# Expert loop of a streaming encoder step: next expert's gate product ahead of this one's down product, lo halves on VectorE alone

## The reference, cut to what matters

```python
def expert_block(args):
    xb, e = args
    return (jax.nn.silu(xb @ w_g[e]) * (xb @ w_u[e])) @ w_d[e]
```

## Time and profile before

| what | value |
|---|---|
| median of 3 runs | 1662.56 us (1661.34 to 1664.23) |
| span of the profiled execution | 1662.2 us |
| TensorE busy | 1306.2 us (79%) |
| VectorE busy | 1166.7 us (70%) |
| ScalarE busy | 694.7 us (42%) |
| GpSimd busy | 925.6 us (56%) |
| moved by DMA | 279.76 MB, mean 168 GB/s |
| the chain that ended last | TensorE 34%, issue 11%, VectorE 8% of the span |

### The profile page before, as it was taken

One profiled execution on the slowest core, in us unless ns is written; L12 is line 12 of the kernel. 1 busy time (PEld: TensorE's weight loads), 2 busy tenths in 40 slices (PEclk: granted clock), 3 DMA queues, 4 the chain that ended last, 5 costly groups with the idle time before them and its releaser, 6 DMA issues.

```text
span 1662.2 us, 18411 instructions
## 1 busy us (share of the span) xinstructions
PE 1306.2 (79%) x5969; PEld 1043.3 (63%) x5969; DVE 1166.7 (70%) x1171; ACT 694.7 (42%) x833; POOL 925.6 (56%) x829
## 2 busy tenths in 40 slices
PE   1777678887755699906888888888888888886998
PEld 0666567675633588805776666766767666744776
DVE  2279969788878422294887998888888789844442
ACT  2322223333323322212665666666666666622121
POOL 1367739999951300043777777777777777730000
PEclk9998889798766799956999999999999999997999
DMA  5311010000010332122898888889999999963320
GB/s 181 109 51 31 12 57 14 24 10 4 28 51 25 127 127 76 38 102 69 291 312 320 301 307 299 303 306 311 326 317 327 318 321 326 330 219 127 123 81 32
DMA packets 122318, 279.76 MB, mean 168 GB/s; under 512 B 17537, under 2 KB 20033, under 8 KB 122269
## 3 DMA queue, kind: packets, MB, share of 16 engines
q1 hardware_dynamic: 112477, 261.28, 45.4%
q0 software_dynamic: 9792, 17.85, 2.9%
HBM read 269.85 MB, written 27.12 MB: 179 GB/s over the span
## 4 chain that ended last, share of the span: by engine, by line
PE 34%; issue 11%; DVE 8%; ACT 2%; DMA 1%; SPq 0%; DVEq 0%; POOL 0%; POOLq 0%; ACTq 0%
PE ps L407 10%; PE ps L408 10%; PE ps L409 10%; DVE ahl L388 2%; PE ps L1615 2%; DVE mem L1538 1%; PE ps L1966 1%; ACT hhl L1075 1%; PE ps L1928 1%; DMA mem<-y_rows 1%; DVE whl L388 1%; PE ps L1862 1%; PE ps L1938 0%; DVE hhl L388 0%; DMA mem<-in_g_ple 0%
## 5 line engine op out<-in xcount | busy, mean ns | idle before, releaser
L388 DVE TENSOR_TENSOR whl<-mem,whl 128x1280 fp32r<-128x1280 f32 (+1 forms) x205 | 506.8, 2503 | 27.1 <-ACT whl L1052 25.7
L388 POOL TENSOR_TENSOR whl<-mem,whl 128x768 fp32r<-128x768 f32 (+1 forms) x213 | 467.7, 2223 | 103.1 <-ACT whl L385 62.1
L407 PE MATMUL ps<-whl,ahl 128*128 128x512 f32 x1124 | 452.9, 403 | 73.5 <-DVE ahl L388 71.4
L1052 ACT ACTIVATE whl<-mem 128x2048 fp32r<-128x2048 f32 x196 | 375.9, 1919 | 178.5 <-PE ps L409 178.5
L408 PE MATMUL ps<-whl,ahl 128*128 128x512 f32 x1124 | 444.6, 396 | 0.0
L409 PE MATMUL ps<-whl,ahl 128*128 128x512 f32 x1124 | 442.8, 394 | 0.0
L407 PEld LDWEIGHTS ps<-whl,ahl 128*128 128x128 f32 x1124 | 221.5, 197 | 128.6 <-issue 71.9
L409 PEld LDWEIGHTS ps<-whl,ahl 128*128 128x128 f32 x1124 | 219.9, 196 | 45.4
L408 PEld LDWEIGHTS ps<-whl,ahl 128*128 128x128 f32 x1124 | 220.5, 196 | 42.6 <-issue 0.2
L459 DVE SCALAR_TENSOR_TENSOR mem<-mem 128x256 f32<-128x256 f32 (+1 forms) x270 | 199.5, 808 | 0.0
L668 POOL TENSOR_SCALAR mem<-mem 128x1 f32<-128x1 f32 (+1 forms) x54 | 21.5, 397 | 318.8 <-ACT mem L875 286.3
(11 more groups left out here) (234 smaller groups left out, 1415.6 us busy)
## 6 DMA issues: line engine op xcount, KB each, us to landing
mem<-in_w_e_up SPq DMA_DIRECT2D x66, 1024.0 KB, 7.5
mem<-in_w_e_down SPq DMA_DIRECT2D x66, 1024.0 KB, 6.8
mem<-in_w_e_gate SPq DMA_DIRECT2D x66, 1024.0 KB, 5.6
mem<-in_x_prompt SPq DMA_DIRECT2D x24, 512.0 KB, 3.4
mem<-y_rows SPq DMA_DIRECT2D x16, 512.0 KB, 5.6
mem<-in_w_in SPq DMA_DIRECT2D x4, 1024.0 KB, 8.7
mem<-in_w_out SPq DMA_DIRECT2D x4, 1024.0 KB, 4.9
h_rows<-mem SPq DMA_DIRECT2D x8, 512.0 KB, 2.6
```

The source lines that it names most:

```text
L388: return which.tensor_tensor(out, full, hi.bitcast(F32), ALU.subtract)
L407: nc.tensor.matmul(out, act_hi, whl[:, 0, w_at], start=first, stop=False)
L1052: nc.scalar.activation(whl[:, 0, slot * CH:(slot + 1) * CH], raw[c], ACT.Copy).then_inc(s_mhi, 1)
```

## The change

- GpSimd makes no lo halves any more; VectorE makes each whole (128x2048), with one counter, also of the first four chunks, which it makes after the slot table. LOV stays in use in the mixer only.
- The jobs run in another order. The gate chunks of expert 0 come first, then for each expert: its up chunks, the next expert's gate chunks, its own down chunks. TensorE's order in an expert becomes: all transposes of the next slots, up, first half of the next gate product, transposes of the hidden row, second half of that gate product, down.
- The gate product goes to bank 2 and bank 7 in turn.
- ScalarE writes all of y in one operation; one counter s_ye takes the place of s_y0 and s_y1.
- The last expert, which has no next, is written out behind the loop. SP loads the chunks in the new order.

The diff, cut to its core:

```diff
+        JOB_CHUNK = (2, 3, 0, 1, 4, 5)
+        JOB_AHEAD = (0, 0, 1, 1, 0, 0)
+        JOB_BUFFER = (2, 3, 4, 5, 0, 1)
+        LAST_JOB = 2 + 6 * (NE - 1)
+        GATE_BANK = (2, 7)
+        def first_job(e):
+            return 6 * e + 2
...
 # SyncE
-            with sp.Fori(1, NE) as e:
-                for c in range(6):
-                    sp.wait_ge(s_mlv, 6 * e + (c - 5))
-                    sp.wait_ge(s_mlp, 6 * e + (c - 5))
-                    sp.dma_start(raw_view(c), expert_chunk(e, c)).then_inc(s_mraw[c], 16)
+            for i in (4, 5):
+                sp.wait_ge(s_mlv, i - 3)
+                load_job(JOB_BUFFER[i], 0, JOB_CHUNK[i])
+            with sp.Fori(1, NE - 1) as e:
+                for i in range(6):
+                    sp.wait_ge(s_mlv, 6 * e + (i - 3))
+                    load_job(JOB_BUFFER[i], e + JOB_AHEAD[i], JOB_CHUNK[i])
+            for i, c in enumerate((2, 3, 4, 5)):
+                sp.wait_ge(s_mlv, LAST_JOB + i - 5)
+                load_job((LAST_JOB + i) % 6, NE - 1, c)
...
 # GpSimd
-            for c in range(4):
-                pool.wait_ge(s_mhi, c + 1)
-                for first, last, signal in ((0, LOV, s_mlv), (LOV, CH, s_mlp)):
-                    lo_part(nc.gpsimd, whl[:, 1, c * CH + first:c * CH + last], whl[:, 0, c * CH + first:c * CH + last],
-                            raw[c][:, first:last]).then_inc(signal, 1)
...
-                    for c in range(4, 10):
-                        expert_lo(6 * e + c, (6 * b + c) % 4, c % 6)
-                    pool.wait_ge(s_y0, e + 2)
-                    pool.wait_ge(s_y1, e + 2)
+                    pool.wait_ge(s_ye, e + 2)
...
 # ScalarE
+            for n in range(4):
+                expert_hi(n, n, n, 16, None)
             slots_hi(0, 1)
+            expert_hi(4, 0, 4, 16, 1)
+            gate_tanh(0, 2, None)
+            act.sem_inc(s_ye, 1)
+            def one_expert(e, b):
+                slots_hi(1 - b, e + 2)
+                for i in (3, 4, 5):
+                    job_hi(e, b, i)
+                hidden_hi(e + 1)
+                job_hi(e, b, 6)
+                gate_tanh(1 - b, first_job(e) + 4, e + 1)
+                for i in (7, 8):
+                    job_hi(e, b, i)
+                weighted_out(e, b, first_job(e) + 6)
...
 # VectorE
+            for n in range(2):
+                expert_lo(n, n, n)
             slots_lo(0, 1)
+            expert_lo(2, 2, 2)
+            expert_lo(3, 3, 3)
+            gated(0, 1)
+            expert_lo(4, 0, 4)
+            def one_expert(e, b):
+                slots_lo(1 - b, e + 2)
+                job_lo(e, b, 3)
+                hidden(first_job(e) + 2, e + 1)
+                job_lo(e, b, 4)
+                hidden_lo(e + 1)
+                job_lo(e, b, 5)
+                job_lo(e, b, 6)
+                gated(1 - b, e + 2)
+                job_lo(e, b, 7)
+                job_lo(e, b, 8)
...
 # TensorE
+            def one_expert(e, b, gathered):
+                slot_transpose(1 - b, 0, gathered=gathered, evacuated=e + 1)
+                slot_transpose(1 - b, 1)
+                up_products(e, b)
+                pe.wait_ge(s_xsl, e + 2)
+                half_product(first_job(e) + 2, (4 + 2 * b) % 4, GATE_BANK[1 - b], 1 - b, 0)
+                hidden_transpose(e)
+                half_product(first_job(e) + 3, (5 + 2 * b) % 4, GATE_BANK[1 - b], 1 - b, 1)
+                pe.wait_ge(s_hl, e + 2)
+                pe.wait_ge(s_ye, e + 1)
+                for half in range(2):
+                    down_product(first_job(e) + 4 + half, (6 + 2 * b + half) % 4, half)
```

More of the change, by code:

```diff
@@ L1045, in _, with expert_hi, job_hi, last_hi @@
             nc.scalar.activation(e2, mt, ACT.Exp).then_inc(s_rta, 1)
[L1048 to L1052, removed]
+            def expert_hi(n, slot, buffer, arrived, free):
+                act.wait_ge(s_mraw[buffer], arrived)
+                if free is not None:
+                    act.wait_ge(s_use, free)
+                nc.scalar.activation(whl[:, 0, slot * CH:(slot + 1) * CH], raw[buffer], ACT.Copy).then_inc(s_mhi, 1)
+            def job_hi(e, b, i):
+                expert_hi(None, (2 + 2 * b + i) % 4, (2 + i) % 6, 16 * (e + (8 + i) // 6), first_job(e) + (i - 3))
+            def last_hi(n):
+                expert_hi(n, n % 4, n % 6, 16 * (n // 6 + 1), n - 3)
             def slots_hi(b, count):
@@ L1056, in slots_hi, with gate_tanh, hidden_hi @@
                 nc.scalar.activation(ahl[:, b, 0, :], banks2(0), ACT.Copy).then_inc(s_xsh, 1)
+            def gate_tanh(b, products, turned):
+                act.wait_ge(s_use, products)
+                if turned is not None:
+                    act.wait_ge(s_mht, turned)
+                nc.scalar.activation(th, bank(GATE_BANK[b]), ACT.Tanh, scale=0.5).then_inc(s_mth, 1)
+            def hidden_hi(turned):
+                act.wait_ge(s_mht, turned)
+                nc.scalar.activation(hhl[:, 0, :], bank(4), ACT.Copy).then_inc(s_hh, 1)
@@ L1065, in _ @@
-            with act.Fori(0, NE, 2) as e0:
-                for b in range(2):
[L1067 to L1082, removed]
+            expert_hi(4, 0, 4, 16, 1)
@@ L1514, in _, with expert_lo, job_lo, last_lo @@
             nc.vector.tensor_copy(idx_gather.bitcast(I32), tmp48).then_inc(s_tab, 1)
[L1517 to L1520, removed]
+            def expert_lo(n, slot, buffer):
+                dve.wait_ge(s_mhi, n + 1)
+                at = slice(slot * CH, (slot + 1) * CH)
+                lo_part(nc.vector, whl[:, 1, at], whl[:, 0, at], raw[buffer]).then_inc(s_mlv, 1)
+            def job_lo(e, b, i):
+                expert_lo(first_job(e) + i, (2 + 2 * b + i) % 4, (2 + i) % 6)
+            def last_lo(n):
+                expert_lo(n, n % 4, n % 6)
             def slots_lo(b, count):
@@ new lines, in gated, with hidden, hidden_lo @@
+            def gated(b, count):
+                dve.wait_ge(s_mth, count)
+                nc.vector.scalar_tensor_tensor(th, th, 1.0, bank(GATE_BANK[b]), ALU.add, ALU.mult).then_inc(s_mg, 1)
+            def hidden(products, count):
+                dve.wait_ge(s_use, products)
+                dve.wait_ge(s_mg, count)
+                nc.vector.tensor_tensor(th, th, bank(3), ALU.mult).then_inc(s_mh, 1)
+            def hidden_lo(count):
+                dve.wait_ge(s_hh, count)
+                lo_part(nc.vector, hhl[:, 1, :], hhl[:, 0, :], bank(4)).then_inc(s_hl, 1)
@@ L1549, in ovf_block @@
+            with dve.Fori(0, NE - 2, 2) as e0:
+                for b in range(2):
+                    one_expert(e0 + b, b)
+            one_expert(NE - 2, 0)
+            last_lo(LAST_JOB + 3)
+            hidden(LAST_JOB + 2, NE)
+            hidden_lo(NE)
+            for n in range(LAST_JOB + 4, LAST_JOB + 8):
+                last_lo(n)
             def ovf_block(j):
@@ L1916, in ovf_block @@
+                    one_expert(e0 + b, b, 8 * e0 + 16 * (1 + b))
+            one_expert(NE - 2, 0, 8 * NE)
+            up_products(NE - 1, 1)
+            hidden_transpose(NE - 1)
+            pe.wait_ge(s_hl, NE + 1)
+            pe.wait_ge(s_ye, NE)
+            for half in range(2):
+                down_product(LAST_JOB + 2 + half, (LAST_JOB + 2 + half) % 4, half)
             def ovf_block(j):
                 if first_extra(j):
-                    pe.wait_ge(s_xsl, NE + 1)
+                    pe.wait_ge(s_g[0], 16 * (NE // 2 + 1))
```

128 lines of the change are left out of this document (52 added, 76 removed).

## The result

The changed kernel takes 1535.9 us in the median of four runs (1532.9 to 1536.7), against 1662.4 before in the same comparison. The ratio is 0.9236, with a 95% interval of 0.9218 to 0.9254: 7.6% faster.

What follows compares the result with a forecast made beforehand. The prediction took TensorE's waits for late lo halves to limit the loop, with DMA the next bound. From 1662.2: -16.2 routing, +2.3 start, -59.2 loop, +2.6 end, plus 0.4 outside the span, gives 1592 us; range 1560 to 1650.

Steps and rivals of the forecast that it cites:

- 348 GB/s is what a share of 1.0 would move: Expert loop: DMA's ceiling taken as rate over share, from 313 GB/s at a share of 0.90.
- DMA's floor is 19.5 us per expert: Expert loop: 6.78 MB an expert needs 19.5 us of DMA, above TensorE's 18.1.
- 3.38 us a chunk: Expert loop: time per loaded chunk at a DMA share of 0.96; 3.25 us at 1.0.
- a packet takes no longer when much is under way: DMA: rate over share stays constant, 348 in the loop, 344 and 355 in two other stretches.
- rival C: Expert loop: TensorE is the bound, as DMA can move more than 348 GB/s; 1537 us, chance 0.12.
- TensorE's pace: Expert loop: TensorE's own work takes 18.1 us an expert, 72 matmuls 16.5 and twelve transposes 1.6.
- Start: Ahead of the loop: routing gains 16.2 us, a lo operation holding GpSimd's copy costs 2.3; first product at 757.0.
- The start of the load queue: Start of the loop: chunk 12 is in 20 us behind the first product, at 777.6, then 179 chunks follow.
- End: Behind the loop: overflow block's weights queue behind five loads of the last stage, +2.6 us, bounds -2.8 and +6.
- D: Expert loop: period stays at 21.66 us, another wait replacing the two; only 13.9 us won, 1649 us, chance 0.06.
- E: Expert loop: whole lo operation takes 4.14 us, VectorE becomes the bound at 28.1 an expert; 1849 us, chance 0.05.
- B: Expert loop: DMA does not fill, share stays at 0.90, TensorE waits for whl; 1631 us, chance 0.22.

Runs made afterwards that it cites:

- VectorE alone: The kernel before in its old order, but all lo halves made whole on VectorE, none on GpSimd: 1584.5 us, ratio 0.9513.
- less compute: The changed kernel without the experts' hi by lo matmul and with only 256 columns of each lo half made in the loop: 1527.5 us.
- half loads: The changed kernel with each load in SyncE's loop cut to its first half, all other work kept: 1529.1 us.
- the run with the gather first: The changed kernel, VectorE's first two lo halves waiting until GpSimd has issued the first gather and copied the second index: 1529.1 us, ratio 0.9180.
- the routing run: The kernel before, only the first four chunks' lo halves moved from GpSimd to VectorE, whole, behind the slot table: 1653.6 us, ratio 0.9936.
- the fastest version: The changed kernel with the first gather issued first, gate and up chunks loaded in 8 KB pieces, slots turned with a stride: 1521.0 us, ratio 0.9148.

## Why the prediction was wrong

**Where it held.** The mechanism of the gain was right: GpSimd's lo halves cost VectorE more than they took off it. VectorE alone gives 80 us, the whole lo half measured 2.29 us against 2.27 forecast, and the waits for ahl and hhl went, as said. By the port lock that the Trainium skill describes ("SBUF — State Buffer", section "SBUF: two separate sides"), the copy would wait out a whole VectorE operation; the trace agrees: the index copy took 2.17 us behind one lo half of 2.24. That TensorE and DMA would be the next two limits was right too; the forecast had DMA alone in front, by 1.4 us an expert.

**The step that failed** is "348 GB/s is what a share of 1.0 would move", and with it "DMA's floor is 19.5 us per expert" and 3.38 us a chunk. What the runs showed in its place is a ceiling of 382 GB/s (less compute), at a share of 1.02. The step rested on "a packet takes no longer when much is under way". It takes less. In the row of the loads' queue q1, share x 16 engines x 500 us / packets is the time of one packet: 113 ns with half loads (share 0.63 of all queues), 109 before (0.88), 106 with VectorE alone (0.97), 102 in the changed kernel and with less compute (1.02). GpSimd's lo halves are not the reason, as the run with half loads has none. The rows for before and after, 800 to 1300 us (packets, MB, share of 16 engines):

```profile
q1 hardware_dynamic: 60515, 143.59, 82.3%
```

```profile
q1 hardware_dynamic: 73731, 174.49, 94.2%
```

So the share is not a linear measure of what is left: from 0.90 at 313 GB/s the step to full was 22%, not 11%. Two parts of it: a full queue shows a share of 1.02, not 1.0, and rate over share rises from 348 to 375. The three rows whose rate I divided by their share all lay below a full queue. Could the trace of before have shown it? It has stretches of 4 us in which the queue was full, and some of them look like the answer:

```profile
1188.00:1192.00 4.00, 4.00 (x20) 3.25 (x19) 3.60 (x4) 3.09 (x2) 0.92 (x1) 1.00 1.02 383
1348.00:1352.00 4.00, 2.69 (x15) 2.22 (x16) 2.62 (x3) 3.15 (x3) 4.00 (x3) 1.00 1.04 378
```

But the same view has others, and a stretch of 20 us can be found that is full all through:

```profile
1148.00:1152.00 4.00, 3.66 (x20) 2.83 (x18) 2.90 (x4) 2.11 (x2) 3.12 (x6) 1.00 1.01 301
...
1303.00:1323.00 20.00, 18.49 (x87) 15.07 (x86) 15.21 (x12) 14.34 (x11) 16.89 (x9) 1.00 1.01 364
```

Of the 150 stretches of 4 us from 800 to 1400 us, 33 have a share of 1.00 or more; they move 301 to 407 GB/s, 359 in the mean. So the trace of before gave 350 to 365 by this way too. It left room above 348, but did not show 382: that took a run in which DMA is the bound throughout.

With 382, DMA's floor is 6.78 MB / 382 = 17.7 us, below the 18.1 that I gave TensorE, and the sum would have been rival C's. C had a chance of 0.12 because of this one reading. That C's 1537 is about 1 us from the measured median is in part luck. Its end of the loop, 1339, was met (1338.4) because three errors cancel: the first product came 2.4 us later, 32 periods are 7 us shorter together, and what the loop takes beside them is 4 us longer. It has nothing of the 5 us won behind the loop. And TensorE was the bound in two thirds of the loop, not in all of it. Why packets get shorter in a full queue no run settles.

**The page.** I weighed 358 GB/s for a core's part against about 425 for a core that streams alone (the Trainium skill, "HBM Reference", section "Specifications (TRN2)"), and found the rows to agree with the first. Neither fits: 382 with pieces of 2 and 4 KB, 400 with longer ones. The kernel runs on one core alone, which is the case the page gives the second figure for; I let my quotient overrule that.

**Terms that were off by less.** TensorE's pace: 18.1 forecast, 17.68 measured (half loads). I took 0.229 us a matmul from a stretch with small pauses and 1.6 for the twelve transposes, which take 0.87 + 0.44 = 1.3 in the changed kernel. Start: -13.9 forecast, -11.5 measured. The routing stretch gave 16.1, as forecast (16.2), and the changed kernel came to it 0.6 us earlier. But I let one lo operation hold the copy (+2.3) and put a late gather outside the sum; both came, 5.2 together, beyond my bound of 4.6. The copy agrees with the page's lock, and the slower issue is VectorE's doing; whether the rest is the starving of which the page warns or the loads in front of the gather is open, as the run with the gather first says. The start of the load queue has a slip: 20 us behind 757.0 is 777.0, not 777.6. End: +2.6 forecast, -3.0 measured. The overflow weights were asked for at 1335.1, when the five PLE loads, issued by 1323.7, had had 11 us; the block's first product then waited for ScalarE's copy and not for weights. That the forecast had a queue there comes in part from the same wrong ceiling; the routing run won 3 us at this place too, with the old order, so not all of the term is explained.

**D and E.** No wait took the place of the removed two; the whole lo half stayed far below 3.1 us. B's share of 0.90 never came.

## What to carry to other kernels

Rate over share at part load is no ceiling: here it was 9% too low, and the short full stretches of the same trace were too scattered to correct it. Measure the ceiling with a run in which everything else is made light, and give a rival more weight where the forecast hangs on one such quotient. Work split between VectorE and GpSimd on operands in SBUF can cost more than it saves: take the split away first, and only then judge an order of work, which here lost 9 us with the split and won 49 without it. After a large gain look for the second limit before working on the first, and look at parts of the loop and not only at its mean: here the two means lay 0.13 us apart, TensorE led in the first twenty experts and DMA in the last eleven, and the fastest version needed longer rows for the loads as well.

## What the runs showed of the hardware that was not expected

A packet of the load queue took 113 ns at a share of 0.63 and 101.6 ns at 1.02: with the same mix of sizes, the time counted for a packet falls as the queue fills. VectorE's subtractions with both inputs in SBUF slow GpSimd's issue of an indirect DMA: 1.04 us in the median before, 2.53 in the changed kernel. The load on DMA is not the reason. With half loads (share 0.63) the issue takes 2.54 in the median. With less compute, where VectorE makes an eighth of each lo half and DMA is full, it takes 1.04. The rows (duration ns min/median/max) are of the changed kernel, half loads and less compute:

```profile
L809 POOL DMA_INDIRECT mem<-h_rows,mem x34: 1013/2532/2547, 747.0 to 1329.8; - x34
...
L811 POOL DMA_INDIRECT mem<-h_rows,mem x34: 1014/2537/2541, 749.4 to 1325.3; - x34
...
L809 POOL DMA_INDIRECT mem<-h_rows,mem x34: 1017/1035/2404, 748.5 to 1325.2; - x34
```

Which step of GpSimd is hit depends on what VectorE runs just then: with VectorE alone in the old order the issue takes 1.03 and the index copy ahead of it 1.80. The landing, in the median 8.3 us after the issue in the changed kernel, is earlier both with half loads (6.3) and with less compute (6.9). Inside the loop, where gathers are issued almost an expert ahead, this costs nothing.
